# Placing weights and activations at different offsets within 128 bytes of on-chip memory

## What is computed

```python
def swiglu(x, w_gu, w_d):
    gate, up = jnp.split(x @ w_gu, 2, axis=-1)
    return (jax.nn.silu(gate) * up) @ w_d
...
    for i in range(DEPTH_2):
        g = norms[i]
        x = x + 0.5 * rms_norm_2(swiglu(rms_norm_2(x, g[0]), ffn_wgu[i, 0], ffn_wd[i, 0]), g[1])
        ...
        x = x + rms_norm_2(mix, g[3])
        x = x + 0.5 * rms_norm_2(swiglu(rms_norm_2(x, g[4]), ffn_wgu[i, 1], ffn_wd[i, 1]), g[5])
```

## Time and profile before

| | |
|---|---|
| median of three runs | 3100.72 us (3099.99 to 3104.38) |
| span of the profiled execution, first to last instruction | 3101.5 us |
| mean granted clock of TensorE | 0.990 of full speed |
| PE busy | 3016.2 us, 97% |
| DVE busy | 2130.9 us, 69% |
| ACT busy | 1528.4 us, 49% |
| transferred | 354.81 MB, mean 114 GB/s |

### The profile page before, as it was taken

The page is one execution under the profiler, slowest core; times in us unless marked ns, Lnnn a source line. Parts: engine busy times, 40 slices in busy tenths (PEclk is TensorE's granted clock), DMA queues, the critical chain, the costliest instruction groups (busy, mean ns, idle before and its releaser), DMA issues.

```text
span 3101.5 us, 49298 instructions
## 1 busy us (share of the span) xinstructions
PE 3016.2 (97%) x19037; PEld 2555.3 (82%) x19037; DVE 2130.9 (69%) x3065; ACT 1528.4 (49%) x2263; POOL 65.0 (2%) x115
## 2 busy tenths in 40 slices
PE   7999999899999999998999999999999999999997
PEld 3888887688779898667878989789988787778996
DVE  5576666899878586775468857786764443588685
ACT  4454645677745354563245535454443332455452
POOL 1000000000000000300000000000000000000000
PEclk9999999899999999999999999999999999999999
DMA  5222222799823332110023232233232222223221
GB/s 226 89 75 76 80 81 83 268 373 379 336 68 109 109 107 89 62 62 19 17 68 102 107 104 102 84 114 109 102 103 82 76 85 78 80 76 123 102 102 68
DMA packets 97101, 354.81 MB, mean 114 GB/s; under 512 B 10896, under 2 KB 11280, under 8 KB 96528
## 3 DMA queue, kind: packets, MB, share of 16 engines
q1 hardware_dynamic: 92448, 334.54, 30.5%
q0 software_dynamic: 3168, 11.54, 1.0%
q10 hardware_dynamic: 1296, 6.11, 0.5%
HBM read 344.27 MB, written 7.86 MB: 114 GB/s over the span
## 4 chain that ended last, share of the span: by engine, by line
PE 89%; DVE 5%; ACT 4%; issue 1%; DMA 1%; POOL 0%; SPq 0%; ACTq 0%; DVEq 0%; POOLq 0%
PE bank L353 13%; PE bank L355 13%; PE bank L354 13%; PE bank L961 7%; PE bank L963 7%; PE bank L962 7%; PE bank L2812 2%; PE bank L2814 2%; PE bank L2813 2%; PE bank L557 2%; PE bank L558 1%; PE bank L562 1%; PE cbank L379 1%; PE bank L3969 1%; PE gbank L1646 1%
## 5 line engine op out<-in xcount | busy, mean ns | idle before, releaser
L325 ACT ACTIVATE whi<-raw 128x1024 fp32r<-128x1024 f32 x310 | 319.3, 1051 | 219.1 <-PE bank L355 182.3
L344 DVE TENSOR_TENSOR wlo<-raw,whi 128x1024 fp32r<-128x1024 f32 x310 | 375.6, 1222 | 70.3 <-ACT whi L325 69.3
L353 PE MATMUL bank<-h_hi_buf,whi 128*128 128x512 f32 x1008 | 410.1, 407 | 8.1 <-DVE h_lo_buf L493 5.1
L355 PE MATMUL bank<-h_hi_buf,wlo 128*128 128x512 f32 x1008 | 394.6, 391 | 0.0
L354 PE MATMUL bank<-h_lo_buf,whi 128*128 128x512 f32 x1008 | 394.2, 391 | 0.0
L353 PE MATMUL bank<-a_hi_buf,whi 128*128 128x512 f32 x832 | 324.9, 390 | 0.5 <-DVE wlo L344 0.5
L354 PE MATMUL bank<-a_lo_buf,whi 128*128 128x512 f32 x832 | 323.7, 389 | 0.0
L355 PE MATMUL bank<-a_hi_buf,wlo 128*128 128x512 f32 x832 | 323.7, 389 | 0.0
L353 PEld LDWEIGHTS bank<-h_hi_buf,whi 128*128 128x128 f32 x1008 | 190.1, 189 | 54.6 <-DVE h_lo_buf L493 6.8
L355 PEld LDWEIGHTS bank<-h_hi_buf,wlo 128*128 128x128 f32 x1008 | 190.0, 188 | 41.3
L354 PEld LDWEIGHTS bank<-h_lo_buf,whi 128*128 128x128 f32 x1008 | 190.4, 189 | 40.2 <-issue 4.1
(11 more groups left out here) (724 smaller groups left out, 7229.1 us busy)
## 6 DMA issues: line engine op xcount, KB each, us to landing
raw<-in_w SPq DMA_DIRECT2D x622, 512.0 KB, 4.0
held<-in_w SPq DMA_DIRECT2D x12, 512.0 KB, 16.5
x<-in_x ACTq DMA_DIRECT2D x2, 2048.0 KB, 11.2
sorted_y<-ysb POOLq DMA_DIRECT2D x6, 512.0 KB, 7.6
token_rows<-hrow POOLq DMA_DIRECT2D x4, 512.0 KB, 4.2
out<-x SPq DMA_DIRECT2D x8, 256.0 KB, 2.0
xc<-in_xc ACTq DMA_DIRECT2D x1, 1024.0 KB, 8.7
sorted_y<-zrow POOLq DMA_DIRECT2D x1, 512.0 KB, 3.1
```

Of the source, the lines that this page charges most:

```text
L325: act.activation(weights(k, g)[0], k.raw[:, g.slot, :], ACT.Copy).then_inc(k.split_hi, 2 * RING + 1 if first == COND_GROUPS * RING else 1)
L344: dve.tensor_tensor(lo, k.raw[:, g.slot, :], hi.bitcast(F32), ALU.subtract).then_inc(k.split_lo, 2 * RING + 1 if first == COND_GROUPS * RI ...
L353: pe.matmul(out, w_hi, hi, start=(t == 0), stop=False)
L355: return pe.matmul(out, w_lo, hi, start=False, stop=(t == tiles - 1))
```

## The change

It alters nothing but the addresses of buffers. Instructions, their order, their waits and their sizes stay.

- The base of the layout goes from a multiple of 64 to a multiple of 2048 (18432). The gap of 1920 bytes in front of it takes `ones`, `ident`, `pair_ones`, `c_in`, `c32`, `c4`, `gain2` and `shift2`.
- `whi` and `wlo` get 32 bytes more than they need and begin 16 bytes into them: `whi` starts 16 bytes behind a multiple of 128, and `wlo` 48.
- `h_hi_buf`, `h_lo_buf` start on a multiple of 128, `a_hi_buf`, `a_lo_buf` and what is placed inside them 32 bytes behind one (`ssq`, `lnv` and `rstd` with them).
- `k.low` and with it `x`, `acc`, `hc`, `whi2`, `wlo2`, `raw2`, the `sum` and `mix` buffers go to multiples of 128.
- The small tables that stood in between move to the end of the memory, and `k.limit` drops by their size (`TAIL`).
- `bump` rounds sizes up to 32 bytes instead of 64.

Offsets within 128 bytes, by buffer:

| buffer | before | after |
|---|---|---|
| `raw`, `h` buffers, `ones`, `ident`, `c4` | 0 | 0 |
| `whi` | 0 | 16 |
| `wlo` | 0 | 48 |
| `a` buffers | 0 | 32 |
| `hc`, `x`, `acc`, `whi2`, `wlo2`, `raw2` | 64 | 0 |
| `mix_hi`, `mix_lo`, `sum_hi`, `sum_lo` | 64 | 0 |

```diff
@@ -4776,6 +4776,9 @@
 
 
 
+TAIL = 32 * -(-VEC_COLS // 8) + 6 * DC * 8 + 2 * (2 * DC * 4) + 4 * 32
+
+
 class Kernel:
 
     pass
@@ -4788,7 +4791,7 @@
     k.moe0 = sum(ph.blocks for ph in phases[:[type(ph) for ph in phases].index(Moe)])
     assert k.moe0 % MOE_RING == 0
     with ExitStack() as ctx:
-        base = -(-nc.sbuf_base // 64) * 64
+        base = -(-nc.sbuf_base // 2048) * 2048
         arena = {}
 
         def sb(name, shape, dt=F32, at=None):
@@ -4798,39 +4801,39 @@
             return t
         k.sb = sb
         KB = 1024
-        at = 0
+        at = -(-nc.sbuf_base // 64) * 64 - base
         def bump(name, shape, dt=F32):
             nonlocal at
             size = int(np.prod(shape[1:])) * (1 if dt == I8 else 4)
             t = sb(name, shape, dt, at=at)
-            at += -(-size // 64) * 64
+            at += -(-size // 32) * 32
             return t
+        def ring(name):
+            t = bump(name, [P, RING * D + 8], F32R)
+            return t[:, 4:4 + RING * D].rearrange("p (s f) -> p s f", s=RING)
+        k.ones = bump("ones", [P, P])
+        k.ident = bump("ident", [P, P])
+        k.pair_ones = bump("pair_ones", [P, P])
+        k.c_in = bump("c_in", [P, DC, 2])
+        k.c32 = bump("c32", [P, DC, 2])
+        k.c4 = bump("c4", [P, DC, 2, 2], F32R)
+        k.gain2 = bump("gain2", [P, DC])
+        k.shift2 = bump("shift2", [P, DC])
+        assert at <= 0
+        at = 0
         k.raw = bump("raw", [P, RING, D])
-        k.whi = bump("whi", [P, RING, D], F32R)
-        k.wlo = bump("wlo", [P, RING, D], F32R)
+        k.whi = ring("whi")
+        k.wlo = ring("wlo")
+        at = -(-at // 128) * 128
         k.h_hi_buf = bump("h_hi_buf", [P, DC, T], F32R)
         k.h_lo_buf = bump("h_lo_buf", [P, DC, T], F32R)
+        at += 32
         k.a_hi_buf = bump("a_hi_buf", [P, DC, T], F32R)
         k.a_lo_buf = bump("a_lo_buf", [P, DC, T], F32R)
         k.ssq = bump("ssq", [P, T])
         k.lnv = bump("lnv", [P, T])
         k.rstd = bump("rstd", [P, T])
-        k.ones = bump("ones", [P, P])
-        k.ident = bump("ident", [P, P])
-        k.eps_col = bump("eps_col", [P, 1])
-        k.vecs = bump("vecs_sb", [P, VEC_COLS])
-        k.pair_ones = bump("pair_ones", [P, P])
-        k.eps2_col = bump("eps2_col", [P, 1])
-        k.tick = bump("tick", [P, 1])
-        k.c_in = bump("c_in", [P, DC, 2])
-        k.c32 = bump("c32", [P, DC, 2])
-        k.c4 = bump("c4", [P, DC, 2, 2], F32R)
-        k.pick = bump("pick", [P, 2])
-        k.mod = bump("mod", [P, 6 * DC, 2])
-        k.gain1 = bump("gain1", [P, 2, DC])
-        k.shift1 = bump("shift1", [P, 2, DC])
-        k.gain2 = bump("gain2", [P, DC])
-        k.shift2 = bump("shift2", [P, DC])
+        at = -(-at // 128) * 128
         k.low = at
         k.x = bump("x", [P, DC, T])
         k.acc = bump("acc", [P, DC, T])
@@ -4839,8 +4842,17 @@
         k.a32 = bump("a32", [P, 2, T])
         k.h32 = sb("h32", [P, 2, T], at=arena["a32"][0])
         k.top = at
+        k.limit = at = (nc.sbuf_usable_end - base - TAIL) // 32 * 32
+        k.eps_col = bump("eps_col", [P, 1])
+        k.vecs = bump("vecs_sb", [P, VEC_COLS])
+        k.eps2_col = bump("eps2_col", [P, 1])
+        k.tick = bump("tick", [P, 1])
+        k.pick = bump("pick", [P, 2])
+        k.mod = bump("mod", [P, 6 * DC, 2])
+        k.gain1 = bump("gain1", [P, 2, DC])
+        k.shift1 = bump("shift1", [P, 2, DC])
+        assert at <= nc.sbuf_usable_end - base
         k.sq0, k.h320 = k.sq, k.h32
-        k.limit = nc.sbuf_usable_end - base
         k.arena = arena
 
         def ps(name, shape):
```

## The result

The changed kernel takes 3143.08 us, the median of 4 runs (3140.83 to 3144.96); the kernel before took 3102.16 us beside it (4 runs, 3099.99 to 3104.38). The ratio is 1.013, with a 95% interval of 1.0117 to 1.0143: some 41 us slower, where 18 us of gain were forecast. The profiled execution's span is 3143.2 us.

What follows compares the result with a forecast made beforehand. PE, 89% of the chain, was taken to bound the kernel through distances between matmul starts. Gains of 15.3, 6.0, 2.0 and 5.0 less 7.7 made 20.6 us, nine tenths of it 18: 3082 us, range 3066 to 3115.

Steps and rivals of the forecast that it cites:

- much faster case: A rival in which the changed kernel gains far more than the forecast; chance 0.04.
- Item 3: 512-column products: `h` by rings from 391 to 389 ns, 6.0 us gained; `a` by rings already free, 0.
- item 1: 256-column products of `h` and `mix` by rings reach 276 ns, 15.3 us gained; at the worst row 6.1 us lost.
- item 6: ACT's block copies, moved tables, lower limit and new base cost nothing; rows can tell apart only offsets within 128.
- Item 2: 256-column products by `sum` go from 278 to 282 or 283 ns, 7.7 us lost; `mix` by `sum` unchanged.
- Items 4 and 5: Context products come down to the free level, 2.0 us gained; experts' products come near it, 5.0 us gained.
- The rival on the slower side: 512-column products lose their free state if 16 apart is as bad as 64 apart: 3129 us; chance 0.13.

Runs made afterwards that it cites:

- the first map: A kernel of its own without the model, 42 groups of 72 matmuls at different operand offsets: means 389 to 397 ns at 512 columns, 276 to 284 at 256.
- the second map: Matmuls alone, model left out, with more offsets and multiples of 256, each group behind 24 matmuls at (0; 96): (0; 256) has 390 ns, (128; 0) 395.
- the last run: The changed kernel with `h` and `a` both at 32 modulo 256, rings at 16 and 48, `sum` and `mix` 64 bytes further: 3108.73 us, ratio 1.0015.

## Why the prediction was wrong

The reading of what bounds the kernel held: no instruction, wait or transfer changed, ACT's and DVE's times stayed, and the matmuls' 45.1 us became 41.7 in the span, 0.92 of them, where nine tenths were taken. That distances depend on placement held as well: in the first map a move of the stationary operand alone, from (0; 0) to (0; 128), took the same matmuls from 389 to 395 ns. In the full kernel, moving buffers alone changed the means of the three `h` groups by 3, 6 and 6 ns, those of the `a` groups by 4, 5 and 9, and the time by 1.3%. No map shows a level below the 276 and 389 ns that the prediction calls free: the best placements have just these, so nothing came of the much faster case that it gave 0.04.

- **Item 3** failed, and it carries the miss. "`h` by rings: 391 against 389 ... 6.0 us gained ... `a` by rings is free already: 0" became 14.9 us lost and 14.9 us lost. The step that failed stands in item 1 and was carried over: that operands an odd number of 16-byte steps apart are at the free level. No row showed it, and what came, 394 to 398, lies around the upper bound of 396. The slip of the modulus in item 6 is not the whole of it: with `h` at 0 as meant, (0; 16, 48), the maps have 395 and 396. The rows of 512 columns stood at the best level of all groups, where 2 ns could be won and 7 lost, and I used the 256-column group for what another distance does. The first map shows 64 apart among the best at 256 columns (276 ns) and 0 apart at 512 (389).
- **Item 6** failed where it said "the offsets within 128 are what the rows can tell apart". They could not tell more, but the second map and the run at 128 from the rings show that the period is 256: (0; 256) has 390 ns and (128; 0) 395, and `h` has 395 in that run. So `a` at "32" was at 160, and the round-up of the base and the padding of the rings was an edit with a price. With `a` at 32 modulo 256, 0 would have been right for it (389 to 391). The table's 64 for `hc`, `sum` and `mix` is 192 modulo 256. By the first map 512 columns tell the two apart, (0; 64) with 395 and (0; 192) with 391; `hc` at 192 by rings at 0 is the distance of (0; 64), and its row had 396. That ACT and the tables cost nothing held (ACT is busy 1527.7 us after 1528.4, and with the new base and tables, all at 0 and the sums at 64, the ratio is 1.0004).
- **Item 1**, 15.3 us gained, came to 0.7 lost: `h` 1.3 gained, `mix` 2.0 lost. Placements 16 or 48 apart lie between 278 and 282 at 256 columns in the maps, and the free 113 ns of the earlier trace rows was reached by 64 apart alone in the maps, and even by that only at times (L137 has 276 in the first map, the same placement 281 in the second).
- **Item 2**, 7.7 lost, held in sign and near in size, 5.8 busy, in part by luck: the change put `h` and `sum` not 0 but 128 apart modulo 256, and that happens to cost as much (282 ns; 0 apart has 283 in the run with everything at 0).
- **Items 4 and 5**, 7.0 gained together, came to 0.8 gained and 1.9 lost.
- Groups that I hadn't listed, `h` by the rings in L557 to L562 and `h` by `a`, add 4.0 us of loss.

These are 14.9 + 14.9 + 0.7 + 5.8 - 0.8 + 1.9 + 4.0 = 41.4 us, less 1.1 for `mix` by `sum`, of TensorE's 45.1; the last 4.8 are spread over small groups. The rival on the slower side is what happened: the 512-column products lost their free state, by more than the "2 to 3 ns each" at which it decides. The distances behind it were not the 16 bytes that it named but 128 and 160 modulo 256 against 16 and 48. It gave 32.6 us for the six groups where 29.8 came, and allowed 9.2 us of gain at 256 columns that did not come; without that gain its sum is 40.3, 36 on the path, against 41. It had a chance of only 0.13, because "an odd step may well avoid what an even one has to find by drifting". That was an argument without a row.

The cause is shown as far as placement goes: undoing the parts brings the time back piece by piece, each against the kernel before run beside it: 16.6 us with the rings, 14.1 with `a`, 8.7 with `sum` and `mix`, and 1.6 are left, within the noise, of 40.9. The first two steps are not pure, since they also shift what lies behind. That the two reads of TensorE meet in the memory is a reading; no run sees the reads themselves. Why (0; 16) ends in one of two states is open.

## What to carry to other kernels

Before operands are moved, look at whether the groups that carry the time are already at the best mean of their form: then a new placement has little to win there, and the bound from the worst group is the price to reckon with. Keep moving and stationary operands of 512-column float32r products 0 apart modulo 256 bytes, both on multiples of 64 ((0; 0), (64; 64) and (128; 128) had 389 here; or test +16, +16, -16, which had 389 to 390), and count every round-up and padding modulo 256. A placement that is good for one width need not be so for the other: (0; 64) had 276 ns at 256 columns in the first map, among the best, and 395 at 512, near the worst. Nor need it be for the other role of the operands: in the last run, with the rings at 16 and 48, `h` and `a` stay at 392 and 390 and the experts' L2813 has 397, against 393 with all at 0 and the sums at 64. A short kernel that maps placements from both a good and a bad state finds the candidates in one run; only the full kernel decides, as both placements with two states, free in a map, were not free in it (395 and 393 ns).

## What the hardware showed that I had not expected

- The period of the placement is 256 bytes: (0; 256) has 390 ns, (128; 0) 395, (0; 0) 389.
- The same placement can run at two rates: (0; 16) with 389 behind (0; 0) and 396 behind (0; 96); (0; 16, 0) with 389 and 396 in two maps, both times behind 24 matmuls of (0; 96). So the products just before it do not decide alone, and what does is not shown. The full kernel took the worse rate for (0; 16), 395.
- In the first map the gap between best and worst placement is 8 ns at either width (389 to 397 at 512 columns, 276 to 284 at 256), so it is not in proportion to the columns; and 0 apart is among the best at 512 (389) and nearly the worst at 256 (283).
- The order of signs matters: (32; 16, 48) has 390 and (32; 48, 16) has 395.
